# A two-layer sparse-attention trunk: the first attention's head started between the last query projections, its loads tied to single stores, its compressed unit's banks released one by one

## The reference, cut

```python
q, kc, vc, ks, vs, kw, vw, gate = split(h @ w_in)         # q, ks, kw rotated; q scaled by 1/8
k_cmp, v_cmp = compress(kc), compress(vc)                 # 63 compressed blocks
s_c = q @ k_cmp;  p_c = masked_softmax(s_c, cmp_end <= t);  o_c = p_c @ v_cmp
s_s = q @ ks;     p_s = masked_softmax(s_s, tok <= t);      o_s = p_s @ vs      # all 16 blocks are selected
s_w = q @ kw;     p_w = masked_softmax(s_w, 0 <= dist < 512);  o_w = p_w @ vw
y = (g0 * o_c + g1 * o_s + g2 * o_w) @ w_out
```

## Time and profile before

| | us |
|---|---|
| median of 3 runs (lowest, highest) | 3291.52 (3285.49, 3293.05) |
| the profiled execution | 3294.07 |
| its span in the trace | 3292.3 |
| busy: PE / DVE / ACT / POOL | 2957.5 / 2047.1 / 1517.5 / 280.0 |
| first layer's last query projection ends, first scores begin | 280.9, 312.87 |
| first layer's attention on PE | 312.87 to 854.1 |

### The profile page before, as it was taken

The page is one execution under the profiler, slowest core; times in us unless marked ns, Lnnn a source line. Parts: engine busy times, 40 slices in busy tenths (PEclk is TensorE's granted clock), DMA queues, the critical chain, the costliest instruction groups (busy, mean ns, idle before and its releaser), DMA issues.

```text
span 3292.3 us, 35560 instructions
## 1 busy us (share of the span) xinstructions
PE 2957.5 (90%) x12424; PEld 2233.6 (68%) x12424; DVE 2047.1 (62%) x3645; ACT 1517.5 (46%) x2624; POOL 280.0 (9%) x221
## 2 busy tenths in 40 slices
PE   7797999999879999999987775679997999999997
PEld 5685656655667888878865664345576788887885
DVE  6545545555267776687766799554426777667666
ACT  4342555555435544454433556344434444444443
POOL 2352000000000000000002134220000000000000
PEclk9887999999989999999998888689998999999998
DMA  5143121121423333333323014341142333333332
GB/s 170 39 101 112 40 59 40 43 56 34 125 64 90 103 90 101 91 94 94 100 64 118 1 54 123 87 128 43 30 135 64 95 92 97 96 95 91 109 99 74
DMA packets 356617, 275.05 MB, mean 84 GB/s; under 512 B 58085, under 2 KB 308007, under 8 KB 355927
## 3 DMA queue, kind: packets, MB, share of 16 engines
q1 hardware_dynamic: 355287, 270.68, 28.1%
q10 hardware_dynamic: 1152, 2.10, 0.2%
HBM read 238.18 MB, written 31.92 MB: 82 GB/s over the span
## 4 chain that ended last, share of the span: by engine, by line
PE 77%; DVE 10%; ACT 4%; DMA 3%; issue 3%; POOL 2%; SPq 1%; POOLq 0%; DVEq 0%; ACTq 0%
PE PS L491 18%; PE PS L492 18%; PE PS L493 18%; PE PS L909 10%; PE PS L830 3%; PE PS L884 3%; PE PS L885 3%; PE PS L890 1%; DVE m_MASK L2304 1%; DVE m_Z L2378 1%; DVE RT_b L596 1%; PE PS L645 1%; DMA WR<-in_nsa_w_out 1%; DMA m_RB<-r_save 0%; PE PS L902 0%
## 5 line engine op out<-in xcount | busy, mean ns | idle before, releaser
L491 PE MATMUL PS<-HH,WH 128*128 128x512 f32 (+1 forms) x2160 | 856.5, 397 | 82.2 <-POOL WL L464 37.6
L492 PE MATMUL PS<-HL,WH 128*128 128x512 f32 (+1 forms) x2160 | 848.1, 393 | 0.0
L493 PE MATMUL PS<-HH,WL 128*128 128x512 f32 (+1 forms) x2160 | 846.7, 392 | 0.0
L491 PEld LDWEIGHTS PS<-HH,WH 128*128 128x128 f32 x2160 | 413.2, 191 | 175.8 <-issue 45.5
L492 PEld LDWEIGHTS PS<-HL,WH 128*128 128x128 f32 x2160 | 413.2, 191 | 86.1 <-issue 2.5
L493 PEld LDWEIGHTS PS<-HH,WL 128*128 128x128 f32 x2160 | 412.5, 191 | 86.4
L480 DVE TENSOR_TENSOR WL<-WR,WH 128x1024 fp32r<-128x1024 f32 x290 | 354.1, 1221 | 112.0 <-ACT WH L473 99.6
L473 ACT ACTIVATE WH<-WR 128x1024 fp32r<-128x1024 f32 x290 | 308.1, 1062 | 123.8 <-PE PS L493 90.5
L929 ACT ACTIVATE n_PX<-PS 128x512 f32<-128x512 f32 (+1 forms) x320 | 172.9, 544 | 223.3 <-PE PS L890 114.1
L1028 DVE CUSTOM_DVE_ANT_0 n_JUNK<-PS,n_MZ 128x512 bf16<-128x512 f32 (+2 forms) x320 | 147.7, 488 | 117.2 <-PE PS L830 117.0
L460 POOL TENSOR_TENSOR TOUCH<-WR 128x1 f32<-128x1 f32 x45 | 12.1, 270 | 1865.9 <-PE PS L493 1025.9
(11 more groups left out here) (374 smaller groups left out, 5152.2 us busy)
## 6 DMA issues: line engine op xcount, KB each, us to landing
WR<-in_ffn_w_up SPq DMA_DIRECT2D x176, 512.0 KB, 3.8
WR<-in_ffn_w_down SPq DMA_DIRECT2D x88, 512.0 KB, 3.6
WH<-qh_save SPq DMA_DIRECT2D x64, 256.0 KB
n_RB<-r_save SPq DMA_DIRECT2D x96, 128.0 KB, 3.0
WR<-in_nsa_w_out SPq DMA_DIRECT2D x16, 512.0 KB, 3.9
WL<-ql_save SPq DMA_DIRECT2D x32, 256.0 KB
WR<-in_dsa_w_in SPq DMA_DIRECT2D x16, 512.0 KB, 4.5
WR<-in_dsa_w_out SPq DMA_DIRECT2D x16, 512.0 KB, 3.8
```

The lines of the kernel that those rows point to most:

```text
L491: nc.tensor.matmul(dst, wh, xh, start=start, stop=False)
L492: nc.tensor.matmul(dst, wh, xl, start=False, stop=False)
L493: return nc.tensor.matmul(dst, wl, xh, start=False, stop=stop)
```

## The change

Nine edits, eight in the first layer, one (the zeroing) in both:

1. Round r of the first layer lies in slot (r + 2) % 3 (`staged`). The slots come free after projections 11, 13 and 15.
2. SP loads round 0 after its store of round 10, round 1 after that of 12, round 2 after that of 14. A load waits for its own round's store (and, in order, for the earlier ones of that parity), not for all.
3. PE makes round 0's 18 peaks six at a time after projections 12, 13 and 14, in banks 0 to 5 (`ring_bank`); DVE reduces them in the same places, between its low part and its addition of the round.
4. The rows of round 0: PE's transpose after projection 15, ACT's copy after its exchange of round 15, SP's two DMAs after the load of round 2 and ahead of the store of round 15. `NM` is cleared at k = 11. The buffers are reordered so that `NM`, `MT`, `CS`, `JUNK` lie over `XF` and `XH`, which are free by then.
5. The first three peaks of round 1 come at step -1, behind the transpose and ahead of the first scores.
6. ACT's first exponentials wait for DVE's and POOL's last products instead of for all stores; the wait for all stores moves ahead of the first copy out (ACT), the first `sums_dve` (DVE), and stays in SP.
7. POOL zeroes `WL`'s rows slot by slot, at k = 13 and 14 and after the last, with a semaphore of its own (`a_zero`), which SP waits for; in the second layer the one memset becomes three.
8. "cmp" units: L902's product waits for all groups but the last to be copied out, only the product of the sums waits for the last; and the two banks are given back one by one.
9. With the slots turned, the output projection's first three weights wait for rounds 14, 15 and 13 where they waited for 13, 14 and 15.

```diff
-            if p.r == 0:
+            if p.r == 0 or x < self.first_peaks + 3:
                 step = -1
...
-            plan.last_done = [(qk, n * plans[0].NU + plans[n].ends[r] + 1) for r in (15, 13, 14)]
+            plan.last_done = [(qk, n * plans[0].NU + plans[n].ends[r] + 1)
+                              for r in ((13, 14, 15), (15, 13, 14))[n]]
...
+            def staged(self, r):
+                return (r + self.turn) % 3
...
+        def ring_bank(a, y):
+
+            return y % 6 if a.n == 0 and y < a.plan.first_peaks else 3 + y % 3
...
-            if a.n == 1:
-                sp.wait_ge(a_saved[r % 2], a.saved0 + 32 * (r // 2 + 1))
+            sp.wait_ge(a_saved[r % 2], a.saved0 + 32 * (r // 2 + 1))
             if r < 3:
-                sp.wait_ge(proj, a.q0 + 2 * PAIRS)
+                sp.wait_ge(proj, a.q0 + (12 + 2 * r if a.n == 0 else 2 * PAIRS))
...
+            if r < 3:
+                sp.wait_ge(a_zero, 3 * a.n + r + 1)
...
+        def early_peaks_pe(pe, a, y0, y1):
+
+            for y in range(y0, y1):
+                if y >= 6:
+                    pe.wait_ge(a_md, a.md0 + a.plan.ring[y - 6][1] + 1)
+                peak_pe(pe, a, y, a.plan.ring[y][1])
...
-                if n.g:
-                    pe.wait_ge(a_ov, a.ov0 + n.g)
+                pe.wait_ge(a_ov, a.ov0 + n.g - 1)
                 nc.tensor.matmul(bank(6), B["VC"][:, g, :], probs, start=True, stop=True)
+                pe.wait_ge(a_ov, a.ov0 + n.g)
                 last = nc.tensor.matmul(bank(7), B["ONB"][:, :], probs, start=True, stop=True)
...
-                nc.scalar.activation(OP[:, slot, :], bank(6), ACT.Copy)
-                nc.scalar.activation(DR[:, slot, :], bank(7), ACT.Copy).then_inc(a_ov, 2)
+                nc.scalar.activation(OP[:, slot, :], bank(6), ACT.Copy).then_inc(a_ov, 1)
+                nc.scalar.activation(DR[:, slot, :], bank(7), ACT.Copy).then_inc(a_ov, 1)
...
+        EARLY_PEAKS = {12: (0, 6), 13: (6, 12), 14: (12, 18)}
...
+                    if k in (10, 12, 14):
+                        load_queries_sp(sp, A0, k // 2 - 5)
+                    if k == 14:
+                        rows_sp(sp, A0, 0)
...
+                if k in EARLY_PEAKS:
+                    if k == 12:
+                        pe.wait_ge(a_ready, a.ready)
+                        pe.wait_ge(S["rl"], 5)
+                        pe.wait_ge(S["rh"], 9)
+                    early_peaks_pe(pe, a, *EARLY_PEAKS[k])
...
+                if k == ROUNDS - 1:
+                    rows_act(act, a, a.plan.first_peaks, 0)
```

More of the change, by code:

```diff
@@ L177, in place_peaks @@
         seen, pending = -1, []
+        self.first_peaks = sum(p.r == 0 for p in self.peaks)
         def put(step, item):
@@ L883, in scores_pe @@
                         masks.append((ii, B["MZ"][:, 0:P]))
-                nc.tensor.matmul(dst, KA[:, g, keys], both_heads(WH, n), start=True, stop=False)
-                last = nc.tensor.matmul(dst, KB[:, g, keys], both_heads(WL, n),
+                nc.tensor.matmul(dst, KA[:, g, keys], both_heads(a, WH, n), start=True, stop=False)
+                last = nc.tensor.matmul(dst, KB[:, g, keys], both_heads(a, WL, n),
                                         start=False, stop=not masks)
@@ L970, in attention_act @@
             plan = a.plan
-            queries_saved(act, a)
+            if a.n == 1:
+                queries_saved(act, a)
             for s in range(-1, plan.steps):
                 if s == -1:
-                    for y in plan.ring_at[-1]:
-                        if plan.ring[y][0] == "rows":
-                            rows_act(act, a, y, plan.ring[y][1])
+                    if a.n == 1:
+                        rows_act(act, a, plan.first_peaks, 0)
+                    else:
+                        act.wait_ge(a_t1, a.q0 + ROUNDS)
+                        act.wait_ge(a_t2, a.q0 + ROUNDS)
                     for u in range(2):
@@ L985, in attention_act @@
                 if s < plan.NU and plan.units[s].last:
+                    if a.n == 0 and plan.units[s].g == 0:
+                        queries_saved(act, a)
                     evict_act(act, a, s)
@@ L1084, in attention_dve @@
                     what, x = plan.ring[y]
-                    if what == "peak":
+                    if what == "peak" and (a.n == 1 or y >= plan.first_peaks):
                         peak_dve(dve, a, y, x)
@@ L1097, in attention_dve, with rows_zero_pool @@
                     output_low_dve(dve, a, r)
+        def rows_zero_pool(pool, a, r):
+            pool.wait_ge(proj, a.q0 + (12 + 2 * r if a.n == 0 else 2 * PAIRS))
+            nc.gpsimd.memset(WL[0:64, a.staged(r), :].bitcast(F32), 0.0).then_inc(a_zero, 1)
         def attention_pool(pool, a):
-            pool.wait_ge(proj, a.q0 + 2 * PAIRS)
-            nc.gpsimd.memset(WL[0:64, :, :].bitcast(F32), 0.0).then_inc(a_ready, 1)
+            for r in range(2 if a.n == 0 else 0, 3):
+                rows_zero_pool(pool, a, r)
             if a.n == 1:
@@ L1879, in prep0_dve @@
                                             ALU.subtract).then_inc(a_qlo, 1)
+                if k in EARLY_PEAKS:
+                    for y in range(*EARLY_PEAKS[k]):
+                        peak_dve(dve, a, y, a.plan.ring[y][1])
                 if k < ROUNDS:
```

81 lines of the change are left out of this document (47 added, 34 removed).

## The result

| | before | changed |
|---|---|---|
| median of the runs, us (lowest, highest) | 3292.24 (3285.49, 3293.05), 4 runs | 3263.4 (3260.45, 3265.64), 4 runs |
| the profiled execution | 3294.07 | 3260.45 |
| its span | 3292.3 | 3258.6 |
| first layer: first scores | 312.87 | 303.69 |
| first layer: first value product | 328.35 | 317.72 |

The ratio is 0.9915, 95% interval 0.9901 to 0.993: 28.8 us less by the medians. The changed kernel was run again later on another chip: 3264.89 us (5 runs) beside 3289.55 (11 runs) of the kernel before, 24.7 less.

The account below looks back on a forecast made before the run. PE bounds the kernel (busy 2957.5 of 3292.3 us), leaving its waits to gain. 12.5 + 1.4 - 1.6 + 15.5 = 27.8 us off 3294.07 gave 3266.3, hence median 3264, within 4 us (0.55); 3257 to 3277 over 8 in 10.

Parts of the forecast that it names:

- First scores, 12.5 less 1.6: Head of the first attention: scores start at 300.4 instead of 312.87, 12.5 us gained, less 1.6 for the clock.
- The stall before the early peaks: After projection 12: PE waits 5.0 us, 264.55 to 269.5, for round 0's load, landing 3.6 us after its last issue.
- The clock's fall: PE's new wait in the projections may bring the clock to 1.2 GHz; 3.2 us at half speed cost 1.6 us.
- SP's steps: Head: SP's queue sets the rows: store 14 at 293.7, rows' second DMA at 297.3, landing 3.1 us later at 300.4.
- Edit 5, 1.4: Round 1 of the first attention: three fewer peaks hold DVE before the first value product; 1.4 us gained, bounds 0 and 2.
- "cmp" units, 15.5 forecast: Steady attention: 8.4 us from L902, 7.5 from the bank give-back, less 0.4 for DVE's waits; bounds 8 and 16.
- rival A: "cmp" units bring little, PE waiting for the exponential or L948 instead; 3272 with half lost, 3279 with all; chance 0.13.
- At nothing: Places counted as costing nothing: output weight 1's split, weight 2's 7.51 us wait, stores' wait, POOL's memset, exponential's table load.
- B: Head's new waits longer: PE waits 8.5 instead of 5.0 us, rows land at 301.6; 3269 us; chance 0.10.
- C: Head: clock doesn't fall in the first wait, rows land in 2.0 us; 1.6 + 1.1 gained, 3261 us; chance 0.12.
- D: Head: rows or round 0's load held by something counted as done, little but "cmp" gain left; 3276 to 3284; chance 0.06.
- E: Slower than before: clock falls in the first wait and stays low through projections 13 to 15 and beyond; 3298; chance 0.04.

Follow-up runs that it names:

- the kernel with both moves: Changed kernel with round 0's load ahead of the last projection weights and store 10, its rows ahead of store 14 and round 2's load: 3254.92, again 3258.86 us.
- the kernel with nine peaks: Changed kernel with nine peaks of round 1 instead of three ahead of the first scores, first layer alone: 3261.04 us, beside 3264.89.

## Why the prediction was right, and where its steps were not

The forecast was 3264 us; 3263.4 was measured. Term by term:

**First scores, 12.5 less 1.6: 10.9 forecast, 9.2 measured.** The stall before the early peaks was 6.20 us, not 5.0: the load held PE until 4.76 us after its last issue, not 3.6. In the eleven traces with an early load this took 4.59 to 5.56. I had read 3.6 from a stretch in which the DMA engines fell quiet, not from a wait that the landing ended; what makes the difference was not tried. The clock's fall cost 1.5 (1.6 forecast). I had read the clock's rows a little wrong: it fell at 286.15 and came back at 876.66, so 5.3 us after PE's stop and 3.5 after its return, not 5.5 and 3.2; and the old load landed at 298.9, not 298.8. Projection 15 then ended 3.4 us later than 289.0: 1.2 of the stall, 1.5 of the clock, and 0.7 more in the early peaks than their 3.1. From there on SP's steps held: store 14 4.35 us later (4.7 forecast), the second rows' DMA 3.8 after it (3.6 forecast), landed after 3.1 (3.1 forecast). But 3.1 was the middle between two bounds.

**Edit 5, 1.4: measured 1.4** (10.6 us at the first value product, 9.2 at the first scores). The list of edits put it into the first layer alone, which was wrong.

**"cmp" units, 15.5 forecast: 10.6 measured in the changed kernel, 11.0 with the edit alone, 12.1 with it taken out.** The mechanism was right and the sum of the waits taken away as well: 16.1 for 15.9. The step that failed is the charge for DVE. I charged 0.4 for its eight waits growing and held that nothing else keeps PE in that stretch; they grew by 3.5 in the kernel with this edit alone. A row of waits that are small before shows what is late now, not how close the next engine follows. That leaves 12.6; the other 0.5 to 2 us show up in no wait. So 3.4 to 4.9 of the 15.5 us were lost, a fifth to a third of what rival A put at stake, and through DVE, not through ACT.

**At nothing.** The third output weight's wait stayed (7.54 for 7.51 us), as said, and so did PE's wait at the start of the second layer (41.1 for 41.9).

**The total.** The steps as measured add up to 21.2 us (9.2, 1.4 and 10.6) instead of 27.8, and the third output weight's first matmul is indeed 21.1 us earlier. The forecast came out all the same, because the medians differ by 28.8 (first runs) and 24.7 us (second chip): 7.6 and 3.5 us more than the steps I had named. No experiment says where these come from; the second layer's peaks may be some of them. After the third output weight the changed kernel's first trace loses 4.0 us up to the second layer's attention, then gains 12.4 in it and 4.2 behind it, and each of these stretches moves by several us from trace to trace. So the exact hit is luck: with every step at its measured size I would have forecast 3270 (3291.52 less 21.2), outside my 4 us.

**The rivals.** B's first half was a third true (6.20 against 8.5). C fell: the clock did fall. D fell: the first trace shows every move at its place. E fell: the clock came back 3.1 us after PE had resumed. In four of the variants this took 5.0 to 6.3 us, so E was nearer than this one trace shows.

## What to carry to other kernels

Where a wait is removed from an engine that two others feed, look at how much room the second one has, not at how long it is waited for now: here 16.1 us less of ACT's waits gave 11, in the main since DVE's went from 3.3 to 6.8. When work is moved forward, put its DMAs in the issuing engine's list by when they are ready and needed: a load behind a store, and rows behind a store and a load, cost some 8 us, which two moved calls gave back. When two single traces differ by more than their steps explain, measure one kernel twice before naming a cause: a stretch of 290 us moved by 2.4 to 3.7 us between two executions of one kernel.

## What the runs showed of the hardware

The granted clock fell sooner than the rows of before had let me expect (4.2 and 5.3 us after PE stopped): in the seven traces with a wait of 6.0 to 6.3 us before the early peaks it fell to 0.50 from 2.1 to 4.5 us after PE stopped. Of the shorter waits there, those of 0.76, 1.28 and 1.68 us left it at 1.00. One of 2.20 did not: PE stood from 265.1 to 267.29, and

```profile
267.00:268.00 1.00, 0.71 (x4) 0.74 (x5) 0.45 (x1) 0.98 (x2) 0.00 (x0) 0.94 1.17 326
268.00:269.00 1.00, 1.00 (x5) 0.81 (x5) 1.00 (x3) 0.18 (x1) 0.43 (x2) 0.50 0.93 356
...
271.00:272.00 1.00, 1.00 (x5) 0.79 (x4) 0.12 (x2) 0.00 (x0) 1.00 (x1) 0.85 0.70 268
```

are of the second trace of the kernel with both moves: the fall comes at 267.9, when PE is at work again, and lasts until 271.3. In the kernel with nine peaks, after a wait of 6.27 us, it lasted from 265.2 to about 275.5. How long the clock stayed down around such a wait differed from 3.4 to some 10 us. Projections 13 to 15 and the early peaks took 20.1 us with the clock up, and 21.6 to 23.0 with it down for part of them.

The second DMA of the rows landed 1.9 to 2.0 us after its issue where no load was issued just ahead of it (six traces), and 2.9 to 3.3 behind a load of 768 KB (eight traces).
